# Second half of the attention's gate projections moved from between its units to a dense block behind the query projections

## What is computed

```python
hn = rmsnorm(h, mix_norm[i])
q, k, v, u, g_attn, g_ssm = jnp.split(hn @ w_in[i], SPLITS, axis=-1)
attn = sliding_window_attention(q, k, v, attn_sinks[i])
y = s5_ssm(u, ...)
y = jax.nn.gelu(y)
ssm = (y @ ssm_glu_a[i]) * jax.nn.sigmoid(y @ ssm_glu_b[i])
merged = jax.nn.sigmoid(g_attn) * attn + jax.nn.sigmoid(g_ssm) * ssm
h = h + merged @ w_out[i]
```

## Time and profile before

| | |
|---|---|
| median of three runs | 4128.43 us (4125.76 to 4130.19) |
| the profiled execution | 4125.97 us, span of the trace 4124.2 us |
| PE busy | 3722.5 us, 90% of the span |
| DVE busy | 1851.9 us, 45% |
| POOL busy | 1531.2 us, 37% |
| ACT busy | 598.5 us, 15% |
| mean granted clock of PE | 0.952 of 2.4 GHz |

### The profile page before, as it was taken

The page is one execution under the profiler, slowest core; times in us unless marked ns, Lnnn a source line. Parts: engine busy times, 40 slices in busy tenths (PEclk is TensorE's granted clock), DMA queues, the critical chain, the costliest instruction groups (busy, mean ns, idle before and its releaser), DMA issues.

```text
span 4124.2 us, 52854 instructions
## 1 busy us (share of the span) xinstructions
PE 3722.5 (90%) x20662; PEld 3162.4 (77%) x20662; DVE 1851.9 (45%) x2660; ACT 598.5 (15%) x1204; POOL 1531.2 (37%) x718
## 2 busy tenths in 40 slices
PE   5977788879999998899999979998888879999997
PEld 2756578668888886899999978887666668888886
DVE  3299566452121217422222286683777762121216
ACT  3132322110000000200000012113443010000000
POOL 3333200354444443444444453322113454444443
PEclk8989899789999999999999989999999989999998
DMA  2110000111111111111111112101002311111111
GB/s 93 36 31 26 21 1 1 61 31 46 51 45 48 45 49 43 30 42 51 41 51 46 40 47 106 55 27 44 29 24 84 117 32 46 51 41 51 46 49 63
DMA packets 56807, 189.86 MB, mean 46 GB/s; under 512 B 6112, under 2 KB 6240, under 8 KB 56032
## 3 DMA queue, kind: packets, MB, share of 16 engines
q1 hardware_dynamic: 45792, 147.20, 11.8%
q10 hardware_dynamic: 10880, 40.78, 2.6%
HBM read 170.05 MB, written 16.84 MB: 45 GB/s over the span
## 4 chain that ended last, share of the span: by engine, by line
PE 73%; DVE 20%; issue 3%; ACT 2%; POOL 1%; DMA 1%; DVEq 0%; POOLq 0%; ACTq 0%
PE acc L560 21%; PE acc L561 21%; PE acc L562 21%; DVE cv_acc L1123 2%; DVE tmp L528 2%; ACT sc L1566 1%; PE acc L846 1%; DVE ssq L648 1%; PE acc L857 1%; DVE st L1790 1%; DVE cvo L1106 1%; PE acc L856 1%; DVE sq L647 1%; PE acc L497 1%; DVE rs L518 1%
## 5 line engine op out<-in xcount | busy, mean ns | idle before, releaser
L449 POOL TENSOR_TENSOR w_hi<-w_raw,consts 128x1024 fp32r<-128x1024 f32 (+3 forms) x316 | 683.8, 2164 | 2127.8 <-PE acc L562 1861.4
L560 PE MATMUL acc<-h_hi,w_hi 128*128 128x512 f32 (+2 forms) x3552 | 1321.3, 372 | 102.4 <-issue 60.0
L561 PE MATMUL acc<-h_lo,w_hi 128*128 128x512 f32 (+2 forms) x3552 | 1320.0, 372 | 0.0
L562 PE MATMUL acc<-h_hi,w_lo 128*128 128x512 f32 (+2 forms) x3552 | 1312.6, 370 | 0.0
L560 PEld LDWEIGHTS acc<-h_hi,w_hi 128*128 128x128 f32 x3552 | 674.3, 190 | 218.5 <-issue 112.5
L561 PEld LDWEIGHTS acc<-h_lo,w_hi 128*128 128x128 f32 x3552 | 672.8, 189 | 103.4 <-issue 2.7
L562 PEld LDWEIGHTS acc<-h_hi,w_lo 128*128 128x128 f32 x3552 | 673.5, 190 | 99.2
L451 POOL TENSOR_TENSOR w_lo<-w_raw,w_hi 128x1024 fp32r<-128x1024 f32 (+3 forms) x316 | 726.0, 2297 | 24.8
L614 DVE TENSOR_TENSOR ff_hi<-tmp,acc 128x512 f32 (+3 forms) x154 | 94.5, 613 | 1119.6 <-PE acc L562 1106.0
L562 PE MATMUL acc<-ff_hi,w_lo 128*128 128x512 f32 (+2 forms) x1232 | 446.8, 363 | 0.0
L560 PE MATMUL acc<-ff_hi,w_hi 128*128 128x512 f32 (+2 forms) x1232 | 446.1, 362 | 0.0
(11 more groups left out here) (301 smaller groups left out, 3647.5 us busy)
## 6 DMA issues: line engine op xcount, KB each, us to landing
w_raw<-in_ffn_w_dram SPq DMA_DIRECT2D x88, 512.0 KB, 3.5
w_raw<-in_w_in_dram SPq DMA_DIRECT2D x56, 512.0 KB, 3.6
w_raw<-in_ffn_w_dram SPq DMA_DIRECT2D x32, 384.0 KB, 3.0
w_raw<-in_w_gate_dram SPq DMA_DIRECT2D x22, 512.0 KB, 3.5
w_raw<-in_w_up_dram SPq DMA_DIRECT2D x22, 512.0 KB, 3.5
w_raw<-in_ffn_w_dram SPq DMA_DIRECT2D x32, 320.0 KB, 2.9
w_raw<-in_w_out_dram SPq DMA_DIRECT2D x16, 512.0 KB, 3.5
gates_kept<-gstage ACTq DMA_DIRECT2D x32, 256.0 KB, 2.0
```

The costliest lines, as they stand in the source:

```text
L449: own.link(pool.tensor_tensor(hi.rearrange(blocks, n=P), raw.rearrange(blocks, n=P), ones.unsqueeze(1).broadcast_to([P, seg.kt, P]), ALU.m ...
L560: pe.matmul(bank, wh, rh, start=(k == 0), stop=False)
L561: pe.matmul(bank, wh, rl, start=False, stop=False)
L562: ins = pe.matmul(bank, wl, rh, start=False, stop=(k == seg.kt - 1))
```

## The change

The four pairs of `at_h` are computed in one block behind `at_q`, by `pe_slab` like any other projection, with two accumulator banks for each buffer. The segment moves ahead of `at_kv` in the plan, so SP's loads and POOL's splits move with it. ACT copies and stores the 16 chunks behind the query chunks, and DVE's wait ahead of the first `c_power` is now for all 16 gate slabs. `gate_piece`, `gates_of` and their calls are gone.

```diff
         add("at_q", 4, KD, CH1, run(t["w_in_2"], 0))
+        add("at_h", 8 - GATES_A, KD, CH1, run(t["w_in_2"], 16 + 2 * GATES_A))
         add("at_kv", 2, KD, CH2, run(t["w_in_2"], 8))
-        add("at_h", 8 - GATES_A, KD, CH1, run(t["w_in_2"], 16 + 2 * GATES_A))
...
-        def gates_of(u):
-
-            total, n = GATE_CHUNKS * KD, len(UNITS)
-            return [divmod(g, KD) for g in range(total * u // n, total * (u + 1) // n)] if u < n else []
...
-            with pe.Fori(0, 4) as i:
-                for j in range(2):
-                    pe_slab(pe, SEG["at_q"], i, j, h)
+            for seg in (SEG["at_q"], SEG["at_h"]):
+                with pe.Fori(0, 4) as i:
+                    for j in range(2):
+                        pe_slab(pe, seg, i, j, h)

             for j in range(2):
-                pe.wait_ge(acc_free[j], SEG["at_q"].q0 + 8)
+                pe.wait_ge(acc_free[j], SEG["at_h"].q0 + 8)
             pe.wait_ge(sem("states_full"), 1)
...
             for u in range(len(UNITS) + 2):
-                for piece in gates_of(u):
-                    gate_piece(piece)
                 if u >= 2:
                     values(u - 2)
...
             for s in range(8):
                 evacuate("at_q", s // 2, s % 2, q2[:, s, :])
+            for s in range(8):
+                for c in range(2):
+                    gate_chunk(SEG["at_h"], s // 2, s % 2, c, c, 3 * (s % 2) + c)
...
             for u in range(len(UNITS) + 1):
-                for f, k in gates_of(u):
-                    if k == KD - 1:
-                        seg, i, j, c = at_chunk(f)
-                        gate_chunk(seg, i, j, c, f % 2, 6 + f % 2)
                 if u:
                     copies(u - 1)
...
             for s in range(2):
-                dve.wait_ge(sem(f"gate_stored{s}"), 16 * 2 * GATES_A)
+                dve.wait_ge(sem(f"gate_stored{s}"), 16 * 16)
             c_power(0)
```

More of the change, by code:

```diff
@@ L1298, in at_bank @@
             return 2 * ((u + 1) % 2)
-        def at_chunk(f):
-            return SEG["at_h"], f // 4, f // 2 % 2, f % 2
-        GATE_CHUNKS = 4 * (8 - GATES_A)
-        def gates_of(u):
-            total, n = GATE_CHUNKS * KD, len(UNITS)
-            return [divmod(g, KD) for g in range(total * u // n, total * (u + 1) // n)] if u < n else []
         def pe_mix2(pe):
@@ L1395, in pe_mix2 @@
             pe.wait_ge(sem("ks_swapped"), 32)
-            def gate_piece(piece):
-                f, k = piece
-                seg, i, j, c = at_chunk(f)
[L1401 to L1412, removed]
-                if k == KD - 1:
-                    ins.then_inc(acc_full[j], 1)
             def scores(u):
```

## The result

The changed kernel takes 4212.44 us (median of four runs, 4210.72 to 4213.62), the kernel before 4127.66 us (four runs, 4125.76 to 4130.19). The ratio is 1.0205, with a 95% interval from 1.0188 to 1.0221: **slower by 84.8 us**. Forecast were +95 us and 4223 us, with a range from 4182 to 4240. The profiled executions took 4213.46 and 4125.97 us; their spans, 4211.7 and 4124.2 us, differ by 87.5 us.

What follows compares the result with a forecast made beforehand. PE's work was 73% of the chain, DVE's 20%; attention units were bound by DVE and ACT. Terms 89.2 − 0.6 − 1.4 − 28.9 + 36.7 = +95.0 us gave 4223 us, range 4182 to 4240.

Steps and rivals of the forecast that it cites:

- The dense block: Behind the query projections: the eight `at_h` slabs, 384 matmuls, run with nothing needed beside them and are paid in full, +89.2 us.
- The seam: From the last projection chunk to the first L1369: PE's earlier start against DVE's wait for the last gate store, −0.6 us.
- The first pieces: Ahead of the attention's first scores: 6 gate matmuls of 0.23 us each go away, −1.4 us.
- The splits: Between attention units: six wide POOL splits at 4.42 us and two narrow at 1.2 move under dense PE work, −28.9 us.
- The clock: In 56 attention units without gate pieces: PE mostly falls to 1.2 GHz and bounds them, 0.8 us more each, +36.7 us.
- Rival 1: In the attention units: PE stays at 2.4 GHz since it never rests long; sum +58.3, 4187 us; chance 0.27.
- Rival 2: In the attention units: clock low all through and loop longer than scaled, 4254 us; 0.05 for results over 4242.
- Rivals 3 and 4: Units get shorter without gate pieces, kernel faster, chance 0.01; or DVE's scan hides part of the new block, under 0.01.

Runs made afterwards that it cites:

- six fillers: Changed kernel plus six matmuls of 512 columns, their products unread, in each attention unit where the gate pieces stood: 4182.94 us.
- three fillers: Changed kernel plus three matmuls of 512 columns, their products unread, in each attention unit where the gate pieces stood: 4183.55 us.
- cut splits: Kernel before, seven of eight splits during the units cut by 128 input features, one part per unit in DVE's pause for ACT's exponentials: 4099.79 us.
- one filler: Changed kernel plus one matmul of 512 columns, its product unread, in each attention unit where the gate pieces stood: 4191.46 us.

## Why the prediction was right and where it missed

*The dense block, +89.2.* Right: 89.0 by start times, and 86.2 to 86.9 us less, seam and all, when it is left out.

*The seam, −0.6.* −1.2, within its bounds of −2.0 and +0.9. DVE's wait for the store came as described (2.7 us from the copy's start to 2816.17). The estimate that its work then takes as long as beside the earlier split was too long: two products took 3.36 instead of 5.30 us, and the way to the first L1359 6.4 instead of 8.3 us.

*The first pieces, −1.4.* −1.65 measured.

*The splits, −28.9.* −29.4 by the kernel with six fillers. The term counted the two intervals at each split and was right to 0.5 us. The dip of the clock in the second short unit of before, 1.4 us, had no term of its own, and makes the −30.8 of the whole stretch.

*The clock, +36.7.* **This is the step that was mis-sized**: it measured 29.7. The mechanism was the one described, PE as the bound of a unit at 1.2 GHz with DVE waiting for L1400, and the loop's length, 4.97 us forecast, came at 4.94. `values` and `scores` took 2.9 us from 3066.63 to their end at 3069.57, and `turn` with its copies the rest. What failed is "I take 4 units in 5 at 1.2 GHz": 33 of 55 intervals were slow, 60%. At their 0.79 us, with 0.26 more for the seven in which the clock fell, they make 27.9 us; the short units of the first block, which I had left as they are, add the other 1.8. That the clock "mostly stays down" was a guess between its two ends, 0 and 45.9 us, since the trace of before had no unit without pieces but the last. The units at the low clock, in which PE hardly rests, got the full clock back after three to seven of them, and those at the full clock lost it again after three.

The spans then differ by 87.5 us where 95.0 were forecast, of which the clock makes −7.0, the splits with that dip −1.9, seam and pieces −0.9, and the executions' own difference ahead of the change +2.2. Between the medians it is 84.8, since the profiled execution of before lay 1.7 us under its median, and that of after 1.0 over.

*Rival 1, the clock holds,* is wrong for this kernel, and right as a price: 4187 us was its time, and the kernels in which the clock is made to hold take 4183. Its span of 4180 to 4195 us was wider than the seam's bounds give, which are 4185 to 4188. The Trainium skill's rule behind it (page "TensorE: Matmul & The Clock Gate", section "Why this matters for your kernels") puts the fall down to long idle gaps. The timeline of after shows PE just ahead of one of the falls:

```profile
2995.41 0.28 PE L1409 MATMUL acc<-consts,sc 128*32 128x128 f32 x1 [0.97 <-DVE sc L1770]
...
2996.96 0.44 PE L1427 MATMUL acc<-pt,vm 128*64 128x128 f32 x4 [0.82 <-ACT pt L1550]
...
2997.76 0.78 PE L1400 MATMUL acc<-ks,q 64*128 64x256 f32 x1
```

Its two pauses are under 1 us (the longest of all full units is 1.04 us), and the scores that follow are at half speed (0.78 us; 0.48 in a unit at full clock). The trace does not agree with that rule, and the measurement decides. Nor is it the length of these pauses that tells the kernels apart: with three fillers PE has the pause of 0.97 us in nearly every full unit, such as this one, and keeps 0.99.

```profile
3004.06 0.28 PE L1409 MATMUL acc<-consts,sc 128*32 128x128 f32 x1 [0.97 <-DVE sc L1779]
```

*Rival 2* had the units low all through (4232 us) or their loop at 5.35 us (4254 us): no run shows either. *Rivals 3 and 4* are out: no full unit is shorter than 4.14 us in any kernel here, and DVE is idle in the block.

Why a change that freed the units of 384 matmuls and eight splits took only 1.1 us off them: it removed 30.8 us, nearly all of it at the splits, and, by the same stroke, the work that had kept PE's clock up, which gave 29.7 back. With the block left out altogether the kernel is at 0.9999 of the time of the kernel before.

What stays open: whether the cut splits would show the same gain in other stages of this kernel, which was not tried; why the clock swings in units that are all alike; and why the first dozen units with one filler stay low when the later ones don't.

## What to carry to other kernels

Dense work in the gaps of a loop that another engine bounds can do more than fill them: here it also kept PE's clock, worth 29.7 us. Before moving such work to a place where it is paid in full, ask what clock the loop has without it, and what its length is at that clock. When two engines get in each other's way, first look at the length of the single instruction and its place against the other's pause; here cutting 2.35 us into 0.46 us and putting it in a pause of 1.08 us took 27 us off, with the same work, 18.7 of them by the cut alone. A price found by undoing (the units with unused matmuls) tells apart two terms that cancel in the trace.

## What the runs showed of the hardware that I had not expected

- In units with no dense work PE's clock swings: 33 slow intervals of 55, in runs of three to seven, with three of 4.15 us between, though each unit does the same work and no pause of PE in the full units is longer than 1.04 us. The Trainium skill's page "TensorE: Matmul & The Clock Gate", in its section "A second HAM failure mode: psum-queue depth-cycling", tells of such swings in a kernel with short pauses between its groups of matmuls. The swings and the short pauses of these rows agree with it; that the pauses are the cause is not shown here, since the kernel with three fillers has such pauses and no swings.
- One unused matmul of 512 columns per unit brought the mean clock of the units from 0.63 to 0.85, three to 0.99, six to 1.00.
- The same pause of PE of 2.72 us behind the first unit is followed by a clock of 0.50 in before and in the kernel with the parts in DVE's pause, and by 1.00 in the one with six fillers.
- POOL's parts of 128 columns beside DVE's scaling cost 0.20 us a unit and not their own 0.94 us.
